# Norm weight as columns in the opening, weight splits of GpSimd in two halves, and shifted positions in a two-layer transformer kernel

## The reference

```
def rms_norm(x, gain):
    xf = x.astype(jnp.float32)
    y = xf * lax.rsqrt(jnp.mean(xf * xf, axis=-1, keepdims=True) + RMS_EPS)
    return (y * gain.astype(jnp.float32)).astype(x.dtype)

hn = rms_norm(x, norm_gain)
proj = jnp.einsum('btd,de->bte', hn, w_in)
```

## Time and profile before

| | |
|---|---|
| median of three runs | 1002.48 us (1002.39 to 1002.74) |
| the profiled execution | 1002.94 us, of which the span of its instructions is 1001.2 us |
| TensorE busy in the span | 975.6 us (97%) |
| VectorE, ScalarE, GpSimd busy | 461.7, 393.0, 390.4 us |
| moved by DMA | 92.54 MB, mean 92 GB/s |

### The profile page before, as it was taken

The page is one execution under the profiler, slowest core; times in us unless marked ns, Lnnn a source line. Parts: engine busy times, 40 slices in busy tenths (PEclk is TensorE's granted clock), DMA queues, the critical chain, the costliest instruction groups (busy, mean ns, idle before and its releaser), DMA issues.

```text
span 1001.2 us, 13229 instructions
## 1 busy us (share of the span) xinstructions
PE 975.6 (97%) x5057; PEld 812.4 (81%) x5057; DVE 461.7 (46%) x955; ACT 393.0 (39%) x727; POOL 390.4 (39%) x302
## 2 busy tenths in 40 slices
PE   9999999999999999989999899999999999999997
PEld 7877877777788878688888888888888888878886
DVE  5574453399654337375458744831211111332224
ACT  4434334256554233335464634433322222343332
POOL 5661441354224434022223035346455444454441
PEclk9999999999999999999999999999999999999999
DMA  7362141211145152051121112233223323322312
GB/s 220 104 191 74 64 137 54 84 43 64 43 165 168 35 169 64 5 185 43 35 93 64 43 43 84 86 115 120 91 84 93 117 84 88 122 84 84 103 66 84
DMA packets 70432, 92.54 MB, mean 92 GB/s; under 512 B 11086, under 2 KB 49523, under 8 KB 70371
## 3 DMA queue, kind: packets, MB, share of 16 engines
q1 hardware_dynamic: 70370, 91.71, 28.4%
HBM read 89.57 MB, written 6.85 MB: 96 GB/s over the span
## 4 chain that ended last, share of the span: by engine, by line
PE 85%; DVE 9%; issue 3%; ACT 2%; POOL 0%; DVEq 0%; POOLq 0%; ACTq 0%
PE psum L1212 64%; PE psum L1498 6%; PE psum L1458 4%; PE psum L1473 3%; PE psum L1308 2%; PE psum L1550 1%; PE psum L1424 1%; PE psum L1269 1%; PE psum L1526 1%; DVE qk_nat L2071 1%; DVE YG L1923 1%; DVE soft L2227 1%; POOL st L2417 0%; PE psum L1511 0%; PE psum L1437 0%
## 5 line engine op out<-in xcount | busy, mean ns | idle before, releaser
L2391 POOL TENSOR_TENSOR WR<-RAW,WR 128x512 fp32r<-128x512 f32 (+3 forms) x268 | 353.7, 1331 | 541.1 <-ACT WR L1647 540.9
L1212 PE MATMUL psum<-WR,XT 128*128 128x512 f32 (+3 forms) x2160 | 517.7, 388 | 1.4 <-DVE actT L2017 0.9
L1212 PEld LDWEIGHTS psum<-WR,XT 128*128 128x128 f32 x2160 | 385.8, 188 | 73.7 <-issue 4.6
L1647 ACT ACTIVATE WR<-RAW 128x512 fp32r<-128x512 f32 (+3 forms) x268 | 159.5, 614 | 241.0 <-PE psum L1212 233.3
L1212 PE MATMUL psum<-XT,WR 128*128 128x512 f32 (+1 forms) x1092 | 241.4, 382 | 0.0
L1212 PEld LDWEIGHTS psum<-XT,WR 128*128 128x128 f32 x1092 | 200.4, 188 | 40.0 <-DVE XT L1998 0.2
L2011 DVE TENSOR_TENSOR gated<-psum,r_bc 128x512 f32<-128x512 f32 x22 | 22.5, 1064 | 168.2 <-PE psum L1212 168.2
L1782 ACT ACTIVATE prob<-prob,st 128x512 f32<-128x512 f32 (+2 forms) x112 | 58.6, 546 | 95.8 <-DVE st L2168 85.4
L1498 PEld LDWEIGHTS psum<-ones_up,probT 128*128 128x128 f32 x536 | 70.5, 191 | 7.2 <-issue 1.8
L1498 PE MATMUL psum<-ones_up,probT 128*128 128x128 f32 x536 | 72.5, 275 | 0.6 <-DVE R L2202 0.4
L2361 DVE TENSOR_TENSOR XT<-actT,XT 128x512 fp32r<-128x512 f32 x22 | 28.3, 1285 | 82.8 <-ACT XT L1838 82.8
(11 more groups left out here) (236 smaller groups left out, 814.6 us busy)
## 6 DMA issues: line engine op xcount, KB each, us to landing
RAW<-in_w_gate_up_dram SPq DMA_DIRECT2D x44, 512.0 KB, 4.7
RAW<-in_w_in_dram SPq DMA_DIRECT2D x13, 1024.0 KB, 5.2
RAW<-in_w_down_dram SPq DMA_DIRECT2D x11, 1024.0 KB, 4.8
RAW<-in_w_out_dram SPq DMA_DIRECT2D x8, 1024.0 KB, 5.2
RAW<-in_w_in_dram SPq DMA_DIRECT2D x14, 512.0 KB, 4.7
rep_scratch<-rows_scratch SPq DMA_DIRECT2D x12, 320.0 KB, 6.5
RAW<-in_w_in_dram SPq DMA_DIRECT2D x4, 768.0 KB, 4.3
R<-in_x_dram SPq DMA_DIRECT2D x8, 256.0 KB, 6.2
```

The lines of the kernel that those rows point to most:

```text
L1212: last = pe.matmul(outp, stationary(x), moving(y), start=start and n == 0, stop=stop and n == 2)
L1647: act.activation(WR[:, s % RING, 0, 0:w], RAW[:, g % 2, q, 0:w], ACT.Copy).then_inc(w_hi, 1)
L2391: pool.tensor_tensor(WR[:, s % RING, 1, 0:w], RAW[:, g % 2, q, 0:w], WR[:, s % RING, 0, 0:w].bitcast(F32), ALU.subtract).then_inc(w_lo, 1)
```

## The change

The opening: the norm's weight is loaded as eight rows of 128 and transposed once, which gives it as eight columns, one for each k-tile ("gain_cols"). x is transposed as it is loaded ("xp"), and the weight is applied when ScalarE and VectorE split the transposed tile, as a factor for each partition. A step "xt" of this phase now is one k-tile over all 512 tokens, not one token tile over four k-tiles. The multiplications at L1903 and the spread row fall away for this phase. The identity and x tiles 2 and 3 (first half) are issued by ScalarE, the others by SyncE; the first two weight tiles get a transfer and a semaphore each. The spins go from 11 matmuls in four places to 6 in two, and are written to another PSUM bank. The sixteen second-half transposes, eight behind k-tile 1 and eight behind k-tile 2 before, now stand in one block behind k-tile 2.

The split of every weight tile on GpSimd is two instructions of half the columns; the semaphore is raised by the second. In `PLAN` and `lags`, eleven numbers change.

```diff
-SPINS = (3, 3, 2, 3)
+SPINS = (3, 3)
+X_ORDER = (0, 2, 1, 3)
...
-PLAN = {'lags': (3, 2, 2, 0, 3, 2, 0, 3, 1, 0, 2, 0, 2, 4, 0, 9, 0, 4, 3, 1, 0, 0, 2, 0, 1, 0, 1), ... 'norm_moba': (104, 8, 3, 15), ... 'qt_sb': (163, 3), ... 'swa': (232, 5, 2, 4, 10), ... 'out1': (66,), ... 'gm_w': (145, 12), ... 'xt_out2': (178, 1), 'out2': (46, 43, 51, 47)}
+PLAN = {'lags': (3, 2, 2, 0, 3, 2, 0, 3, 2, 0, 1, 0, 2, 4, 0, 8, 0, 4, 3, 1, 0, 0, 2, 0, 1, 0, 1), ... 'norm_moba': (104, 8, 3, 18), ... 'qt_sb': (162, 3), ... 'swa': (232, 5, 2, 5, 10), ... 'out1': (69,), ... 'gm_w': (142, 13), ... 'xt_out2': (182, 1), 'out2': (46, 43, 51, 45)}
...
-    tl.extend([("zero", "fox"), ("spin", 0), ("gain_row", 0), ("spin", 1)])
-    tl.extend([("gx", "in1", 0, 0), ("gx", "in1", 1, 0), ("xt", "in1", 0, 0), ("gx", "in1", 2, 0), ("gx", "in1", 3, 0), ("xt", "in1", 1, 0)])
-    tl.extend([("spin", 2), ("xt", "in1", 2, 0), ("split", 0), ("xt", "in1", 3, 0), ("gain_row", 1), ("spin", 3)])
-    tl.extend(("split", s) for s in (1, 2, 3))
-    tl.extend(("gx", "in1", t, 1) for t in range(2))
+    tl.extend([("zero", "fox"), ("spin", 0), ("gain_cols",)])
+    tl.extend(("xp", "in1", t, 0) for t in X_ORDER)
+    tl.extend([("spin", 1), ("split", 0), ("xt", "in1", 0, 0), ("xt", "in1", 1, 0), ("split", 1)])
+    tl.extend([("xt", "in1", 2, 0), ("xt", "in1", 3, 0), ("split", 2), ("split", 3)])
...
+            if (c, k) == (0, 2):
+                tl.extend(("xp", "in1", t, 1) for t in X_ORDER)
+                tl.extend(("xt", "in1", q, 1) for q in range(4))
...
-            sp.dma_start(gain_row[0:1, :], a["norm_gain"]).then_inc(s_gain, 16)
+            sp.dma_start(gain_rows[0:KD, :], a["norm_gain"].rearrange("o (k n) -> (o k) n", k=KD)).then_inc(s_gain, 16)
             load_x(0, 0)
-            sp.dma_start(ident[:, :], c["ident"]).then_inc(s_ident, 16)
-            for t in range(1, NT):
-                load_x(t, 0)
+            load_x(1, 0)
...
+                elif what == "gain_cols":
+                    pe.wait_ge(s_ident, 16)
                     pe.wait_ge(s_gain, 16)
-                    pe.matmul(XB[hf], ones_up[0:1, 0:1].broadcast_to([1, P]), gain_row[0:1, 512 * hf:512 * hf + 512],
-                              start=True, stop=True).then_inc(gain_rows, 1)
+                    pe.transpose(MM[1][:, 0:KD], gain_rows[0:KD, :], ident[0:KD, 0:KD]).then_inc(gain_cols, 1)
+                elif what == "xp":
+                    _, phase, t, hf = step
+                    pe.wait_ge(s_x[t][hf], 16)
+                    for q in range(4):
+                        k = 4 * hf + q
...
+                        last = pe.transpose(XB[q][:, P * t:P * t + P], R1[:, t, P * k:P * k + P], ident[:, :])
+                        if t == X_ORDER[-1]:
+                            last.then_inc(xt_in, 1)
...
+            act.dma_start(ident[:, :], c["ident"]).then_inc(s_ident, 16)
+            for t in (2, 3):
+                act.dma_start(R1[:, t, 0:512], x_rows[:, t, 0:512]).then_inc(s_x[t][0], 16)
...
+                    act.activation(XT[:, 4 * hf + q, 0, :], XB[q], ACT.Copy, scale=gain[0][:, 4 * hf + q:4 * hf + q + 1]).then_inc(xt_hi, 1)
...
+                    dve.scalar_tensor_tensor(out=XT[:, 4 * hf + q, 1, :], in0=XB[q], scalar=gain[0][:, 4 * hf + q:4 * hf + q + 1],
+                                             in1=XT[:, 4 * hf + q, 0, :].bitcast(F32), op0=ALU.mult, op1=ALU.subtract).then_inc(xt_lo, 1)
...
-                    pool.tensor_tensor(WR[:, s % RING, 1, 0:w], RAW[:, g % 2, q, 0:w], WR[:, s % RING, 0, 0:w].bitcast(F32),
-                                       ALU.subtract).then_inc(w_lo, 1)
+                    for lo, hi in ((0, w // 4 * 2), (w // 4 * 2, w)):
+                        last = pool.tensor_tensor(WR[:, s % RING, 1, lo:hi], RAW[:, g % 2, q, lo:hi],
+                                                  WR[:, s % RING, 0, lo:hi].bitcast(F32), ALU.subtract)
+                    last.then_inc(w_lo, 1)
```

More of the change, by code:

```diff
@@ L694, in hybrid_two_block_kernel @@
         s_x = [[sem(f"x_landed{t}_{hf}") for hf in range(2)] for t in range(NT)]
-        s_first = sem("first_two_weight_tiles_landed")
+        s_first = [sem(f"first_weight_tile_landed{n}") for n in range(2)]
         s_gain = sem("gain_landed")
@@ L979, in xt_bank @@
             _, phase, t, hf = step
-            if (phase, hf) in (("in1", 0), ("out1", 0), ("out2", 1)):
+            if (phase, hf) in (("out1", 0), ("out2", 1)):
                 return ("mm", t)
@@ L1272, in _ @@
                         last.then_inc(cmp_in, 1)
-                elif what == "xt":
+                elif what == "xt" and step[1] != "in1":
                     _, phase, t, hf = step
@@ L1382, in _ @@
                     for t in tiles:
-                        if ch == 0 and n % 4 == 0 and phase != "gu":
+                        if ch == 0 and phase == "in1":
+                            if t == 0:
+                                pe.wait_ge(xt_lo, nth["xt", phase, n % 4, halves(phase)[n // 4]] + 1)
+                            if (n, t) == (0, 1):
+                                pe.wait_ge(gain_copied, 1)
+                        elif ch == 0 and n % 4 == 0 and phase != "gu":
                             pe.wait_ge(xt_lo, nth["xt", phase, t, halves(phase)[n // 4]] + 1)
@@ L1647, in _ @@
                     act.activation(WR[:, s % RING, 0, 0:w], RAW[:, g % 2, q, 0:w], ACT.Copy).then_inc(w_hi, 1)
-                elif what == "gain_row":
-                    hf = step[1]
-                    act.wait_ge(gain_rows, hf + 1)
-                    act.activation(gain[0][:, 512 * hf:512 * hf + 512], XB[hf], ACT.Copy).then_inc(gain_copied, 1)
+                elif what == "gain_cols":
+                    act.wait_ge(gain_cols, 1)
+                    act.activation(gain[0][:, 0:KD], MM[1][:, 0:KD], ACT.Copy).then_inc(gain_copied, 1)
+                elif what == "xt" and step[1] == "in1":
+                    _, _, q, hf = step
+                    act.wait_ge(xt_in, nth[step] + 1)
+                    if (q, hf) == (0, 0):
+                        act.wait_ge(gain_copied, 1)
+                    act.activation(XT[:, 4 * hf + q, 0, :], XB[q], ACT.Copy, scale=gain[0][:, 4 * hf + q:4 * hf + q + 1]).then_inc(xt_hi, 1)
                 elif what == "xt":
@@ L1992, in _ @@
                     last.then_inc(cmp_out, 1)
+                elif what == "xt" and step[1] == "in1":
+                    _, _, q, hf = step
+                    dve.wait_ge(xt_hi, nth[step] + 1)
+                    dve.scalar_tensor_tensor(out=XT[:, 4 * hf + q, 1, :], in0=XB[q], scalar=gain[0][:, 4 * hf + q:4 * hf + q + 1],
+                                             in1=XT[:, 4 * hf + q, 0, :].bitcast(F32), op0=ALU.mult, op1=ALU.subtract).then_inc(xt_lo, 1)
                 elif what == "xt":
```

49 lines of the change are left out of this document (18 added, 31 removed).

## The result

The changed kernel takes 992.88 us in the median (992.69 to 993.06), the one before 1002.46 in the same series: ratio 0.9902, 95% interval 0.9887 to 0.9916. That is 9.6 us faster. The forecast was 998.1 with a range from 995.8 to 1001.4: the right sign, less than half the size. The profiled execution took 993.06 us, its span 990.8. Two single executions further down were slow (1390.66 us in e9, 3449.43 in e11); each shifts its median by 0.04 us.

The account below looks back on a forecast made before the run. TensorE, busy 975.6 of 1001.2 us, was taken to bound the kernel. Opening 1.6, halves 1.8 and positions 1.0 sum to 4.4 us, from 1002.94 to 998.5, or 998.1 against the median; range 995.8 to 1001.4.

Parts of the forecast that it names:

- the halves: GpSimd's weight splits in two instructions let VectorE in sooner: 1.8 us gained, bounds +1 (slower) and -3.5.
- the opening: Start-up before the first product, moved from 12.68 to 10.45 us: 2.2 gained, 0.6 lost to the clock, net 1.6.
- the positions: Eleven moved plan numbers cover two waits on "issue" (1.2 and 0.9 us): 1.0 us gained, bounds +1.0 and -2.1.
- the landing of the first weights: In the opening, the first weight tile lands at 8.2 us, the middle between 7.5 and 8.95.
- The clock's 0.6: In the opening, TensorE's low clock after the first product costs 0.6 us, bounds nothing and 3.2.
- The suffix sums: TensorE's two waits at L1526 (1.7 and 1.4 us at the longest) shrink by 0.6 each, 1.2 in all.
- The one behind YG: The 1.2 us wait at L1308, behind four YG instructions held about 1 us too long, gives 1.0.
- losses in GpSimd's queue: Longer splits delay GpSimd's power for the norm, and VectorE elsewhere meets two halves for one: 0.9 us subtracted.
- A: Rival: TensorE's first products run at 1.2 GHz for 6 us, 3.2 lost instead of 0.6: 1000.7 us; chance 0.12.
- B: Rival: GpSimd's second half takes the port again at once, so the halves don't release VectorE: 1000.8 us; chance 0.10.
- C: Rival: the norm's chain through GpSimd gets slower, up to 0.7 us per tile: 1008.3, or 1004.1 us; chance 0.08.
- D: Rival: x lands no earlier, products start at 11.2 or later: 998.9 us; counted within the forecast's case, 0.64.

Follow-up runs that it names:

- e9: Changed kernel with weight splits in quarters up to the feed-forward, halves from there on, and eight spins for three at the start: 992.52 us.
- e11: Kernel before with one number changed, the transposes of the second output product due four quarters later (178 to 182): 1001.11 us.
- e6: Changed kernel with all loads of x and the identity issued by SyncE again, in the old order: 994.04 us.
- e8: Changed kernel with eight spins for three at the start: 991.97 us.
- e1: Kernel before with the new opening only, whole weight splits and old positions: 999.60 us.
- the mirror image: Changed kernel with each weight split as one whole instruction again: 997.56 us.
- e2: Kernel before with GpSimd's weight splits in two halves only: 998.12 us.
- e7: Changed kernel without the three spins in front of the first product: 994.21 us in the median, 992.31 in the profiled execution.
- e5: Changed kernel with every weight split in four instructions of a quarter: 994.19 us in the median, 992.47 in the profiled execution.
- e12: Changed kernel with quarter splits only from the first projection's fourth chunk up to the feed-forward, halves elsewhere, eight spins for three at the start: 990.55 us.

## Why the prediction was wrong, point by point

The mechanisms were right, and the sum failed in the sizes of its terms: the halves by most (1.8 us for 4.5), then the opening (1.6 for 3.1) and the positions (1.0 for 2.15).

- **What bounds the kernel.** Right: TensorE, the opening, and waits behind VectorE instructions that GpSimd holds up. No wait for a split appeared in the changed kernel.
- **The opening, 1.6 us forecast, 3.1 measured alone.** The failed term is the landing of the first weights. The prediction took 8.2, the middle between full effect (7.5) and none (8.95) of the earlier issue, "so that part of an earlier issue is lost in the line". The copy started at 7.49, the end with full effect; e6 gives 1.2 of 1.4 us for the issue alone. From there the sum was right: 0.71 to GpSimd, 1.41 for two halves (1.50 forecast). Then 0.45 more until the product, because VectorE's part ended at 9.9 and the spins, at the low clock, at 10.1; the prediction had the weights as the later branch. The clock's 0.6 was 0.45 in the changed kernel (36 products in 8.91 us against 8.46 in e8) and 0.1 to 0.2 in e1. And e1's trace has 0.5 us from the wait at 62 us, which the sum had counted under the halves and of which it isn't shown that the opening removes it.
- **The halves, 1.8 us forecast, 4.5 alone and 4.7 in the mirror image.** The mechanism was right, the size wrong by three terms. The suffix sums were priced at 0.6 for one instruction of the chain; there are two held ones, 2.2 us in all for 1.2. The gains at 117, 242 and 450 us (0.49, 0.46, 0.56) weren't in the sum at all: the prediction priced six of the waits and took the small ones as fixed. The one behind YG was priced at 1.0 and gave 1.3. And 0.9 was subtracted for losses in GpSimd's queue. Behind the first product the ledger of e2 shows none. Its first product is 0.59 late, but e11 with whole splits is 0.34 late as well, and in the new opening the start varies more (9.60 to 10.06 with three spins) than the halves could explain. What the halves do cost is the 0.4 us outside the span, for which the sum took the 1.7 of before as fixed. A split of 512 columns got longer by 1.41 - 1.27 = 0.14 undisturbed, near the lower bound of 0.13, and by 0.26 in the mean (two halves of 0.815 us against 1.37).
- **The positions, 1.0 forecast, 2.15 alone.** Of the two "issue" waits the one at L1308 went, and gave the 1.2 it stood for (1.35 net in e11). The one at L1613, 0.9, stayed: it stands in front of "gm", whose position didn't change. The step moved forward is "gm_w", which is L1604 and which the text ahead of the prediction puts at L1613 as well; moving it cost 0.5 at 523 us. The half that was missing, 0.7 at 209 and 0.7 at 271 to 277, came from moves that the prediction called without a large wait; which of the other numbers does it, no run separates.
- **The rivals.** A (the clock stays low) didn't come in the changed kernel: two products ran at the low level, not 6 us of them. But e7 has executions 2 us longer with fewer spins, without a trace of them. B fell: turns are taken between two halves without a semaphore between them. C, GpSimd's queue ahead of the norm, wasn't seen with halves, and is what e5 and e9 show with quarters: 1.9 us of wait for 1.5, with GpSimd's power for the norm (L2437) starting 0.7 us later against TensorE's products than in the changed kernel. D fell (10.06).
- **The signs named beforehand.** First product between 9.8 and 11.2 (10.06), suffix-sum waits under 1.2 and 0.9 (0.5 in all), no "issue" wait at L1308 and GpSimd about 450 us busy (449.6) were right. YG instructions were expected near 1.2 us, which is what they had before in the mean; they came to 0.87 in e2, as theory A of that run had it.
- **The range.** The forecast added best guesses for each part and then pulled each to the careful side: half of the landing, 0.9 off for losses nobody had seen, half of the positions. Three terms that err the same way add; the bounds it had itself worked out (2.9, 3.5, 2.1) sum to 8.5, and 9.6 lies a little beyond even them. The range should have reached to their sum.

## What to carry to other kernels

An engine off the critical path can hold up one that is on it by the length of its single instructions, not by its load: cut its long instructions where it has pauses, and leave them whole where it has none (quarters won at 208, 253 and 442 us and lost in the two stages where GpSimd had hardly a break). When a chain of held instructions ends in a wait, price every instruction of the chain. Compare two traces by the start of the n-th matmul of the common work: the jumps of the lead say where each microsecond was won, which a table of waits can miss (0.46 us at 242, where the wait in the table stays at 0.78), and only the level before and behind a stretch counts, not the peak inside it.

## What the runs showed of the hardware

- A cast on VectorE with a single SBUF input and SBUF output is held by GpSimd as an instruction with two inputs is: L2232 took 1.80 us beside whole splits and 1.25 beside halves at the place shown, and 1315 and 1038 ns in the mean of its four. The prediction looked for two-input instructions only. The Trainium skill ("SBUF — State Buffer", Who interferes with whom) names casts among the operations that can take the shared port pair; the trace agrees, with these 0.55 us.
- VectorE gets in between two GpSimd instructions that follow each other without a wait, at the cost of GpSimd: 5.28 us for three halves of 0.7.
- The same pause of 1.9 us of TensorE was followed by 1.00 of the clock in one trace and by 0.67 over 5 us in another, at a price of some 1.6 us (the lead fell by 2.0 in e9 and by 0.4 in e5).
- In the opening TensorE's clock rose at different times behind the same work. After 3 spins and a pause of 2.0 to 2.4 us it was still at 1.2 GHz when the products began in the changed kernel (10.06), and at 2.4 GHz from 7.8 us on in e7 and from about 8.3 in e5, where the six records of the spins take 0.83 us instead of 1.48. After 8 spins and hardly a pause all three traces (e8, e9, e12) were at 2.4 GHz before 7.1 us. So more spins brought it up earlier each time, but fewer didn't always leave it low.
